# Experts as quads of four 32-row units in column groups, and decay rows spread by transfers, in a two-layer hybrid decoder step

## The reference

```python
# mLSTM, one chunk (the kernel uses chunks of 128 rows), per head
b = cumsum(log_forget)
log_d = where(causal, b[:, None] - b[None, :] + ig[None, :], -inf)
m_t = maximum(b + m, max(log_d, -1))
d = exp(log_d - m_t[:, None])           # the decay matrix
s = (q @ k.T) * d

# mixture of experts: 32 experts in 4 groups, each token goes to 2 of the 8 of one group
for each expert e:                      # rows of the tokens that chose e
    h = silu(x_e @ e_gate[e]) * (x_e @ e_up[e])      # 1024 -> 256
    y_e = h @ e_down[e]                              # 256 -> 1024
out[token] = sum of weight * y over its two experts
```

## Time and profile before

| | |
|---|---|
| median of 3 runs | 2792.8 us (2783.36 to 2795.58) |
| the profiled execution's own time | 2790.42 us |
| its span, from the first to the last instruction | 2788.3 us |
| busy in it: PE, weight loads, DVE, ACT, POOL | 2543.1, 1403.2, 1199.7, 707.0, 245.2 us |
| mean granted TensorE clock | 0.949 |
| moved by transfers | 502.24 MB, mean 180 GB/s |

### The profile page before, as it was taken

One profiled execution on the slowest core, in us unless ns is written; L12 is line 12 of the kernel. 1 busy time (PEld: TensorE's weight loads), 2 busy tenths in 40 slices (PEclk: granted clock), 3 DMA queues, 4 the chain that ended last, 5 costly groups with the idle time before them and its releaser, 6 DMA issues. The chain is left out here.

```text
span 2788.3 us, 37700 instructions
## 1 busy us (share of the span) xinstructions
PE 2543.1 (91%) x12344; PEld 1403.2 (50%) x12344; DVE 1199.7 (43%) x2946; ACT 707.0 (25%) x1440; POOL 245.2 (9%) x347
## 2 busy tenths in 40 slices
PE   7999978878989999999599998786799999999987
PEld 3555545554554444444255555454555544544443
DVE  3444446645752122222345544564466512322225
ACT  2555444422210000000145554443321100000002
POOL 0000028000002000000000000740000110000002
PEclk9999989988989999999799999998899899999998
DMA  7222156433206279999553312653231163999956
GB/s 270 75 72 63 52 144 167 101 123 117 86 19 264 103 278 369 364 366 362 219 165 94 98 54 72 180 144 89 113 137 42 62 267 116 369 367 369 368 214 270
DMA packets 238260, 502.24 MB, mean 180 GB/s; under 512 B 67190, under 2 KB 151166, under 8 KB 212744
## 3 DMA queue, kind: packets, MB, share of 16 engines
q1 hardware_dynamic: 199528, 397.58, 41.2%
q0 software_dynamic: 15856, 53.11, 5.4%
q10 hardware_dynamic: 22720, 49.55, 4.6%
HBM read 390.24 MB, written 109.90 MB: 179 GB/s over the span
## 5 line engine op out<-in xcount | busy, mean ns | idle before, releaser
L474 PE MATMUL pj_zp<-pj_w,pj_xT 128*128 128x512 f32 (+1 forms) x1280 | 505.2, 542 | 3.6 <-DMA pj_w<-in_w_in 2.8
L2128 PE MATMUL op_bank<-ex_wgu,ex_xT 128*128 128x512 f32 x1024 | 455.8, 598 | 3.9 <-DVE ex_xT L2538 3.9
L474 PEld LDWEIGHTS pj_zp<-pj_w,pj_xT 128*128 128x128 f32 x1280 | 225.6, 192 | 202.8 <-issue 193.9
L2128 PEld LDWEIGHTS op_bank<-ex_wgu,ex_xT 128*128 128x128 f32 x1024 | 192.2, 193 | 222.3 <-issue 217.6
L2019 PE MATMUL op_bank<-op_wout,op_hT 128*128 128x512 f32 x512 | 238.6, 626 | 1.5 <-issue 1.5
L2138 PE MATMUL op_bank<-ex_wd,ex_hT 128*128 128x512 f32 x512 | 230.5, 593 | 2.0 <-DVE ex_hT L2556 2.0
L2062 PE MATMUL op_bank<-op_wpg,op_hT 128*128 128x512 f32 x512 | 226.5, 601 | 0.0
L2544 DVE TENSOR_TENSOR ex_h<-ex_sil,op_bank 128x256 f32<-128x256 f32 x64 | 26.9, 421 | 424.7 <-ACT ex_sil L2254 424.7
L2254 ACT ACTIVATE ex_sil<-op_bank 128x256 f32<-128x256 f32 x64 | 24.5, 383 | 697.8 <-PE op_bank L2128 697.8
L2019 PEld LDWEIGHTS op_bank<-op_wout,op_hT 128*128 128x128 f32 x512 | 102.5, 204 | 125.9 <-issue 123.5
L2062 PEld LDWEIGHTS op_bank<-op_wpg,op_hT 128*128 128x128 f32 x512 | 98.8, 193 | 123.2 <-issue 123.0
(11 more groups left out here) (425 smaller groups left out, 3326.5 us busy)
## 6 DMA issues: line engine op xcount, KB each, us to landing
ex_wgu<-in_e_gate SPq DMA_DIRECT2D x64, 1024.0 KB, 7.0
ex_wgu<-in_e_up SPq DMA_DIRECT2D x64, 1024.0 KB, 9.7
ex_wd<-in_e_down SPq DMA_DIRECT2D x64, 1024.0 KB, 11.6
h<-scratch_XR SPq DMA_DIRECT2D x64, 512.0 KB, 3.9
scratch_YR<-ex_y ACTq DMA_DIRECT2D x64, 512.0 KB, 8.8
pj_w<-in_w_in SPq DMA_DIRECT2D x8, 2048.0 KB, 18.0
pc_ckv<-in_cache_ckv SPq DMA_DIRECT2D x256, 64.0 KB, 1.9
cv_cch<-scratch_Z POOLq DMA_DIRECT2D x48, 256.0 KB, 4.2
```

The costliest lines, as they stand in the source:

```text
L474: last = pe.matmul(zp[c % ZB][:, 0:cn], xT[:, t % 2, k, :], w[:, k, c0:c0 + cn], start=(k == 0), stop=(k == KC - 1), skip_group_check=True)
L2128: last = pe.matmul(gu[s % 2], xT[:, s % 2, c, :], wgu[s][:, :, c, :], start=(c == 0), stop=(c == KC - 1))
```

## The change

Two things are changed.

**Decay rows.** PE's `decays(u)` is gone. SP stores `a` (2 KB) to a scratch tensor in DRAM, waits for that to land, and loads it back into all 128 partitions at once (256 KB) into a new tile `decays`, which DVE's `decay(u)` reads in place of PSUM.

**Experts.** Each expert has 96 places at a fixed address of `XR` and `YR` (row `96 * e`), so the 32 experts fill 24 groups of 128 rows, called quads here; a quad is four units of 32 rows, and its units belong to one or two experts. The gate, up and down products of a quad are done unit by unit, each unit in its own 32 columns of the array with its own expert's weights. All 24 quads are written out in the program, with fixed addresses; the loop and its branches are gone. Rows beyond 96 of an expert go to a general loop behind (`rest_turns`), whose turns run one after another without overlap; it has room for 22 blocks and runs `used` of them, which is none when no expert has over 96 rows. SP loads gate and up matrices, down matrices and rows in an order sorted by the quad that frees their place. The first two experts are loaded as soon as all rows of `h1` are made. Since places that get no row are read too, POOL zeroes `XR` wholly and `YR` from row 3072 in the first layer's projection phase: 62 stores where there were 4.

```diff
+UNIT, UNITS = 32, 3
+CAP = UNIT * UNITS
+QUADS = NE * CAP // P
+REST = NE * CAP
+BLOCKS = 2 * (SEQ + DECB) // (CAP + 1) + 1
+XROWS = REST + 2 * (SEQ + DECB) + P
...
+                    if is_chunk(u):
+                        sp.wait_ge(a_ready, u + 1)
+                        sp.dma_start(d["DECAY"], a[:, :]).then_inc(a_kept, 16)
+                    if t < TP:
                         if 4 * t < cache.COUNTS[0]:
                             cache.load(sp, d, layer, 4 * t, 4, 0)
                     if is_chunk(u):
+                        sp.wait_ge(a_kept, 16 * (u + 1))
+                        if u:
+                            sp.wait_ge(e_out, u)
+                        sp.dma_start(decays[:, :, :].rearrange("p h n -> p (h n)"),
+                                     d["DECAY"].rearrange("(o h) n -> o (h n)", o=1).broadcast_to([P, NH * P])).then_inc(a_spread, 16)
                         sp.wait_ge(k_out, 2 * u + 2)
...
+                    for r in range(0, XROWS, P):
+                        if r % (8 * P) == 0:
+                            pool.wait_ge(o_ready, min(r // (8 * P) + 3, NT))
+                        n = min(P, XROWS - r)
+                        pool.dma_start(d["XR"][r:r + n], zero[0:n, :]).then_inc(zero_stored, 16)
+                        if r >= REST:
+                            pool.dma_start(d["YR"][r:r + n], zero[0:n, :]).then_inc(zero_stored, 16)
...
-                def decays(u):
-                    pe.wait_ge(a_ready, u + 1)
-                    for h in range(NH):
-                        last = pe.matmul(f[2][:, h * P:(h + 1) * P], headrow[:, h, :], a[:, :], start=True, stop=True)
-                    last.then_inc(a_done, 1)
...
+def first_quad(e):
+    return UNITS * e * UNIT // P
...
+def last_quad(e):
+    return (UNITS * (e + 1) - 1) * UNIT // P
...
+def experts_of(q):
+    return [(4 * q + j) // UNITS for j in range(4)]
...
+def rest_turns(eng, used):
+
     with eng.Fori(0, -(-BLOCKS // SLOTS)) as r:
         with eng.If(SLOTS * r < used):
             for i in range(SLOTS):
...
+                with eng.If(SLOTS * r + i < used):
+                    yield SLOTS * r + i
...
+                todo = [(last_quad(e - SLOTS) + 0.5, 0, load_gate_up, e) for e in range(SLOTS, NE)]
+                todo += [(last_quad(e - SLOTS) + 1.5, 1, load_down, e) for e in range(SLOTS, NE)]
+                todo += [(q - XSLOTS - 0.5, 2, load_rows, q) for q in range(XSLOTS, QUADS)]
+                for _, kind, load, n in sorted(todo, key=lambda a: a[0:2]):
+                    if kind == 0:
+                        sp.wait_ge(gu_done, last_quad(n - SLOTS) + 1)
+                    elif kind == 1:
+                        sp.wait_ge(y_all_done, last_quad(n - SLOTS) + 1)
+                    else:
+                        sp.wait_ge(tp_done, 2 * (n - XSLOTS) + 2)
+                    load(n)
...
+                def gate_up(q):
+                    pe.wait_ge(xT_dve, 2 * q + 2)
+                    for e in range(NE):
+                        if first_quad(e) == q:
+                            pe.wait_ge(gu_in[e % SLOTS], 32 * (e // SLOTS + 1))
+                    for c in range(KC):
+                        for part, s in units(q):
+                            last = pe.matmul(gu[q % 2][part], xT[:, q % 2, c, part], wgu[s][:, :, c, :], start=(c == 0), stop=(c == KC - 1),
+                                             skip_group_check=True)
+                    last.then_inc(gu_done, 1)
...
+                rows_turned(0)
+                for q in range(QUADS):
+                    gate_up(q)
+                    if q + 1 < QUADS:
+                        rows_turned(q + 1)
+                    if q:
+                        down(q - 1)
+                    hidden_turned(q)
+                down(QUADS - 1)
...
+                for s in range(2):
+                    dve.wait_ge(stored[s], 16 * (QUADS // 2))
                 dve.wait_ge(tab_loaded, 16)
                 used = dve.value_load(tab[0:1, TOTAL:TOTAL + 1], min_val=0, max_val=BLOCKS)
```

More of the change, by code:

```diff
@@ L1754 @@
 SLOTS = 4
[L1757 to L1768, removed]
+XSLOTS = 4
+def first_quad(e):
[5 more added lines that the diff above has]
+def rest_turns(eng, used):
     with eng.Fori(0, -(-BLOCKS // SLOTS)) as r:
@@ L1929, in _, with load_rows, load_gate_up @@
                         out.load_weights(sp, d, layer, wpg, "w_pg", wpg_loaded)
+                def load_rows(q):
+                    sp.dma_start(xe[:, q % XSLOTS, :], d["XR"][rows(q)]).then_inc(x_in[q % XSLOTS], 16)
+                def load_gate_up(e, src=None, done=None):
+                    s = e % SLOTS
+                    for n, w in enumerate(("e_gate", "e_up")):
+                        sp.dma_start(wgu[s][:, n].rearrange("p k n -> p (k n)"),
+                                     d[w][layer, e].rearrange("(p k) n -> p (k n)", k=KC)).then_inc(gu_in[s], 16)
@@ L1952, in _ @@
-                sp.wait_ge(h1_ready, NT)
-                for b in range(2):
-                    load_weights(expert_of(b), b)
-                first = row_of(0)
-                sp.wait_ge(base_ready, 1)
-                sp.wait_ge(scattered, SCATTERS * (layer + 1))
-                load_rows(first, 0)
-                for b in range(1, SLOTS):
-                    row = row_of(b)
-                    sp.wait_ge(base_ready, b + 1)
-                    load_rows(row, b)
-                sp.wait_ge(g_done, 2 * 6)
@@ new lines, in hidden_turned, with down @@
+                def hidden_turned(q):
+                    pe.wait_ge(h_ready, q + 1)
+                    for c in range(2):
+                        last = pe.transpose(htp[q % 2][:, c, :], he[:, q % 2, c::2], ident[:, :])
+                    last.then_inc(ht_done, 1)
+                def down(q):
+                    if q:
+                        pe.wait_ge(y_dve, 2 * q)
+                    pe.wait_ge(hT_ready, q + 1)
+                    for e in range(NE):
+                        if first_quad(e) == q:
+                            pe.wait_ge(wd_in[e % SLOTS], 16 * (e // SLOTS + 1))
+                    for n in range(2):
+                        for c in range(2):
+                            for part, s in units(q):
+                                last = pe.matmul(yp[n][part, :], heT[:, q % 2, c, part], wd[s][:, c, n * 512:(n + 1) * 512], start=(c == 0), stop=(c == 1),
+                                                 skip_group_check=True)
+                        if n == 0:
+                            last.then_inc(y_done, 1)
+                    last.then_inc(y_all_done, 1)
@@ L2150, in _ @@
+                    pe.sem_inc(rest_free, 1)
             @block.scalar
@@ L2243, in _, with stored_rows @@
                 stored_base(NT - 1)
-                for s in range(2):
-                    act.sem_inc(stored[s], 16)
+                def stored_rows(q):
+                    act.wait_ge(y_dve, 2 * q + 2)
+                    act.dma_start(d["YR"][rows(q)], ye[:, q % 2, :]).then_inc(stored[q % 2], 16)
+                for q in range(QUADS):
+                    act.wait_ge(gu_done, q + 1)
+                    act.activation(sil[:, q % 2, :], gu[q % 2][:, 0, :], ACT.Silu).then_inc(sil_done, 1)
+                    if q:
+                        stored_rows(q - 1)
@@ L2263, in _ @@
-                overlapped_turns(act, used, turn)
+                for b in rest_turns(act, used):
+                    row = act.value_load(tab[0:1, ds(4 * b + 1, 1)], min_val=0, max_val=XROWS - P)
+                    act.wait_ge(rest_gu, b + 1)
+                    act.activation(sil[:, 0, :], gu[0][:, 0, :], ACT.Silu).then_inc(rest_sil, 1)
+                    act.wait_ge(rest_out, b + 1)
+                    act.dma_start(d["YR"][ds(row, P)], ye[:, 0, :]).then_inc(rest_stored, 16)
                 for s in range(2):
@@ L2561, in combine_last @@
+                    dve.wait_ge(rest_y, b + 1)
+                    dve.wait_ge(rest_stored, 16 * b + 16)
+                    for n in range(2):
+                        last = dve.tensor_copy(ye[:, 0, n * 512:(n + 1) * 512], yp[n][:, :])
+                    last.then_inc(rest_out, 1)
 def combine_last(nc, d, layer, ident):
```

236 lines of the change are left out of this document (116 added, 120 removed).

## The result

The changed kernel takes 2624.0 us (median of four, 2622.8 to 2628.3), against 2790.1 us before: 0.941 of it (95% interval 0.938 to 0.943), 166 us less. The forecast was 2672 us; the time lies at the lower edge of the range, where the rival "the queue goes faster when it is never empty" stood with 2624. The profiled execution took 2624.26 us, its span is 2622.4 us.

What follows compares the result with a forecast made beforehand. The prediction took PE to set the pace before, transfers nearly full, and the expert stages to turn transfer-bound at 381 GB/s. Stages -105.4, decays -17.4, ends +5: -118 on 2790.4 us gave 2672 us, range 2624 to 2715.

Steps and rivals of the forecast that it cites:

- the queue goes faster when it is never empty: Rival for the expert stages: transfers reach 423 GB/s, 77 us a layer saved, 2624 us in all; chance 0.12.
- PE bound before; two resources nearly full: Old expert stages: PE sets the pace at 11.43 us a block, transfers busy 0.96 to 0.97 at 360 to 367 GB/s.
- I take 381: New expert stages: transfers run at 381 GB/s, the mean of four full stretches, with 360 and 423 as bounds.
- at 423, 77 us a layer: The faster-queue rival's step: at 423 GB/s each layer's expert stage gets 77 us shorter.
- The stage turns transfer-bound: Expert stage: three quads take 41.3 us of transfers against 34.3 of PE; 52.7 us a layer saved, 105.4 in all.
- The gate-up after a wait: Expert stage, behind PE's last wait: the gate-up takes 9.88 us instead of 7.03, so 2.85 us are added.
- Column groups: Expert products on PE: four units with different weights run side by side, a quad's gate-up taking about 7.3 us.
- Changes of mode: Quads on PE: four changes between narrow and full products at 0.1 us each, 0.4 us a quad, hidden behind transfers.
- Decay rows: Projection phase: dropping PE's four decay products saves 1.09 us in each of 16 chunks, 17.4 us.
- The cover at PE that the prediction named: Projection phase: queries are rotated 6.6 us before PE asks for them, which can cover late decay rows.
- The end of the stage: After the last quad: DVE's wait for stores and six skipped turns come in a row, 2.5 us a layer, 5 in all.
- Routing and zeros at nothing: Seven small DVE operations ahead of the scatter and 62 zero stores in the first layer's projection phase cost nothing.

Runs made afterwards that it cites:

- The light PE in the kernel before: The kernel before with four of the eight chunks of the gate and up products, all transfers kept; a block took 9.95 us at 421 GB/s, the stage 316.6 us.
- the run with fewer bytes: The changed kernel with experts from the fifth on loading only half of their down matrix; the first layer's stage took 292.1 us.
- the run alone: The kernel before with only the decay rows by transfers added; 2763.4 us, 0.991 of before.
- the expert half alone: The changed kernel with the decay products on PE again, its routing and zero stores kept; 2648.9 us, 0.949 of before.
- half of the changes away: The changed kernel with the hidden rows' transposes ahead of the down products, two changes of mode a quad instead of four; stages 297.7 and 297.4 us.
- full width: The changed kernel with each quad's gate, up and down products 128 wide by one expert's matrices; first layer's stage 293.7 us, whole time 2645 us.
- the light changed kernel: The changed kernel with four of the eight chunks of the gate and up products, all transfers kept; the stage took 281.6 us.

## Why the prediction was nearly right, and where it was off

The forecast lay 48 us beside the measured time. It held 0.70 for a stage near 381 GB/s, 2640 to 2705 us, and 0.12 for a faster queue; 2624.04 us is inside the stated range only because the range was drawn down to that rival's 2624. That it lies inside is luck.

*PE bound before; two resources nearly full.* Right for PE. "The transfers have almost nothing in reserve" is the sentence that failed, and with it the step **"I take 381"**: the four stretches of the earlier trace rows were read as a limit, and they were PE's demand. The light PE in the kernel before shows 421 GB/s with everything else unchanged, the run with fewer bytes shows the same 0.96 to 0.99 where reserve is certain. The Trainium skill, "Perfetto Trace Analysis", section Identifying the Most-Contended Engine, says that occupancy is misleading for transfers and that their throughput should be read against the memory's peak. The traces agree that the share misleads: 364 and 420 GB/s both look full. The Trainium skill, "HBM Reference", section Specifications (TRN2), puts a core that streams alone at about 425 GB/s. That is 1% above what ten kernels reached here (420 to 422).

*The rival "the queue goes faster when it is never empty".* Its time, 2624, came out, and so in the main did its reason, that the queue was slow because PE let go late: with a light PE the old loop gives 421. What the runs add is that the new order of loads is not needed for that. Its step "at 423, 77 us a layer" measured 73.5.

*The stage turns transfer-bound.* Half right. Where the transfers run full, three quads take 37.4 us of bytes against 36.3 of PE, not 41.3 against 34.3; "PE waits some 7 us in three quads" was 0.8 to 1.1, though the last wait did come at quad 21 as worked out. But PE waits for no weights before the 16th quad, so for most of the stage its own pace counts, and the transfers add 2.9 us to it.

*The gate-up after a wait.* The 2.85 us added for it were not paid: behind waits of 0.8 to 1.1 us it took 7.07, at a granted clock of 1.00. The 9.88 at 977.12, from which the term was taken, has its like in the changed kernel's first gate-up, 9.83 at a granted clock of 0.72.

*Column groups.* Right: 7.07 us for a quad's gate-up, 7.3 forecast.

*Changes of mode.* 0.4 us a quad were forecast from one pair of rows. Narrow products cost 0.67 in all; leaving out two of the four changes gave 0.2, a tenth each as forecast. Whether the rest is the other two changes or the narrow products themselves stays open.

*Decay rows.* 17.4 forecast; 20.1 between the two traces, 19.5 in the run alone. Without the products a tile is 1.28 us shorter, and not 1.09: the forecast took the time from the first product to the next group and left out that the groups beside it get shorter too (the scores 1.16 before, 1.05 after). "No wait of DVE for `decays`" was wrong: it waits 4.08 us in the tile shown, and 1.93 at the same place in the kernel that has no zero stores. The cover at PE that the prediction named held.

*The end of the stage.* 2.5 us a layer forecast, 2.9 and 3.2 measured; that the wait ahead of the turns makes most of it is shown by the run that moves it. The forecast named over 10 us between last result and next phase as a sign of being wrong; 10.07 were measured, from 7.20.

*Routing and zeros at nothing.* The zeros: no cost that shows, by the expert half alone. The routing was not tried by itself; the stages start 8.4 us sooner, which is the decays' 9.1 less 0.8.

Of the 48 us by which the forecast was too slow, 41.7 lie in the two stages, 2.7 in the decays, 4.8 in other phases, less 1.1 for the ends. In the first stage's 20.9 us the rate is the term that was mis-sized: 93.3 MB at 420 in place of 381 GB/s take 222.1 us, 22.8 less. Behind the last wait 39.5 us pass in place of 42.3, mostly for the 2.85 that were not paid. Against that, the last wait ends 257.1 us after the first gate-up, 4.5 later than the forecast's sum gives with 420.

## What to carry to other kernels

A rate seen under an engine that is always busy can be that engine's demand: before taking it for a limit, take work off the engine in one run and read the GB/s then. Where two resources are within a few per cent of each other, relieve both or expect little from one. Here 3.4 us less work for PE in each of 24 quads, 82 us in all, left the pace of three quads where it was, at 37.45 us, and shortened the stage by 15; 13% fewer bytes shortened it by 4.5. A wait that moves ahead of a loop that does not run is paid in full, so it belongs inside the turns that need it.

## What the runs showed of the hardware

The transfers of one core, loads and stores mixed in pieces of 0.5 to 1 MB, level off at 420 to 422 GB/s over stretches of 50 us in all ten kernels here that let them, by the old order and the new; the busy share there reads 1.01 to 1.02, and 0.96 to 0.99 already at 360 to 387 GB/s.

Work behind a wait of PE can be slower than the same work in the flow, and where it is, the granted clock of its stretch is lower. A gate-up behind a wait of 2.74 us with half of the changes away, one behind 2.80 us at full width, one behind 5.70 us in the light changed kernel, and one behind 0.83 us in the changed kernel:

```profile
1148.78:1157.55 8.77, 8.77 (x65) 2.89 (x65) 0.00 (x0) 0.00 (x0) 0.00 (x0) 0.81 1.03 425
```

```profile
1183.00:1191.60 8.60, 8.52 (x18) 3.89 (x19) 0.00 (x0) 0.00 (x0) 0.00 (x0) 0.83 1.03 427
```

```profile
1175.58:1181.83 6.25, 6.25 (x33) 1.66 (x33) 0.00 (x0) 0.00 (x0) 0.00 (x0) 0.58 1.03 428
```

```profile
1151.00:1158.10 7.10, 7.05 (x65) 2.44 (x65) 0.00 (x0) 0.00 (x0) 0.00 (x0) 1.00 1.01 418
```

The time times the clock is that of the flow: 8.77 x 0.81 = 7.1, 8.50 x 0.83 = 7.1, 6.25 x 0.58 = 3.6 (3.64 in the flow). It does not follow from the wait alone: two other gate-ups at full width, behind 2.78 and 2.80 us, took 7.10 and 7.11.

The mixing phase of the second layer, which no edit touches, before and after:

```profile
2015.00:2173.00 158.00, 151.94 (x553) 82.64 (x553) 103.25 (x184) 30.19 (x53) 0.00 (x0) 0.93 0.25 86
```

```profile
1923.00:2075.00 152.00, 146.11 (x552) 79.23 (x552) 103.26 (x184) 30.01 (x53) 0.00 (x0) 0.97 0.26 89
```

The same work took 158 us at a granted clock of 0.93 and 152 at 0.97. Over all the runs it was 151.9 to 159.1 us, and 5 us of a difference between two single executions can be no more than that.
